# Five heads of one tile's queries moved in among the attention work of three later tiles, with the forget gates cut in two and the gelu issued sooner

## The chip, the core and the metric

The kernel runs on one core of a Trainium2 chip. The core has five engines with a queue of instructions each: TensorE (PE, matrix products into the eight PSUM banks), VectorE (DVE), ScalarE (ACT), GpSimd (POOL, which here issues the gathers) and SyncE (SP, which here issues the loads of weights). Each engine runs its own list in order and stops at a semaphore that isn't there yet. The metric is the device time of one execution in microseconds (us), as a median of several executions.

## The reference

One block of a transformer on 512 tokens of width 1024: two kinds of attention side by side, an output projection, and then, for each token and each of 8 heads, a retrieval of 16 of 16384 single-neuron experts. Cut to what matters:

```python
proj = rmsnorm(x, norm1_g) @ w_in                 # qa, ka, va, forget gates fa, qb, kb, vb
log_f = log_sigmoid(fa + b_f)                     # 8 heads; its running sum biases the logits
out_a = forgetting_attention(qa, ka, va, log_f)   # 8 heads, causal
out_b = differential_attention(qb, kb, vb, lam)   # 4 heads, two maps each, chunk-causal
h = x + concat(out_a, out_b) @ w_out
hn = rmsnorm(h, norm2_g)
q = (hn @ w_q).reshape(tokens, 8, 2, 128)         # per head: two queries of 128
sc = q . sub_keys                                 # 2 x 128 scores; top 16 of each side, then of their 256 sums
eidx, g = 16 experts and their softmax weights    # per token and head
h += sum_k gelu(u[eidx_k] . hn) * g_k * v[eidx_k] # u, v: tables of 16384 rows of 1024
out = rmsnorm(h, final_g)
```

## The kernel before

The 512 tokens are 4 tiles of 128. A head of a tile needs 16 rows of the table u and 16 of v for each token, gathered by POOL: 0.5 MB for each such row of 128 tokens, a "pair" of a u row and a v row being 1 MB. The kernel has three stages.

**Alone.** Tile 0 goes through attention and output projection; then the first three heads (0 to 2) of its queries are made. The list of this stage is BEFORE, which ends with ("keys", 0, 2).

**Hosted.** The retrieval for heads 0 to 6 of tile 0 runs on DVE: for each row a dot product (L1536) and, two groups later, a multiply and add into h (L1572). Woven into it is everything else: the rest of tile 0's queries and the whole attention of tiles 1 to 3 (group 1). A head is 4 groups of 4 rows, and each group has 9 gaps; a place is written here as head.group.gap, so 0.3.3 is gap 3 of group 3 of head 0. In the even gaps 0, 2, 4, 6 DVE does a dot, in the odd ones an add; then every engine does its part of the pieces that the planner has put into that gap. The planner gives each piece a share (share()) and spreads the list `later` over 27 x 9 gaps by the running sum of the shares. In the list of before, heads 3 to 7 of tile 0's queries stand first and the pieces of group 1 behind them.

**Rows.** From head 7 of tile 0 on, u and v come as one 1 MB row each (L710), DVE does the dot alone, ACT makes a diagonal of the weights, and PE adds the rows up (L993). 25 heads of 16 rows go this way.

The pieces that matter here. ("project", 1, s, q): a product with one of the 12 slabs of w_in for tiles 1 to 3; slabs 0 to 3 and 6 to 9 are queries and keys (16 matmuls of 384 columns, L785), 4, 5, 10 and 11 values (a piece for each tile, L777). ("query", 0, c): for an even c a product of h's turned tile with 256 columns of w_q (L777), which ACT copies into `staged`; for an odd c two transposes out of that copy (turn(), L806). ("keys", 0, hd): the scores of head hd (L896). ("forget", 1): PE makes the product with the gates' 8 columns (L836); DVE adds the bias (L1353), takes the magnitude (L1356) and waits for ACT, which does exp and ln, each with a table load of its own (L1164, L1167); then DVE goes on with the decay: subtract, running sum and two copies (L1358 to L1364). ("selq", 1, t) and ("attend", 1, half, step) use that sum: PE makes the scores (L928, L932), DVE adds the mask and finds the maximum (L1440), ACT takes the exponential (L1194), PE turns the map and multiplies it with the values.

ACT's list in the hosted stage has one more thing: the gelu of a group's four dots (L1219), issued in gap 4 of the next group behind the pieces of gaps 0 to 3, and the softmax of the next head's weights (gate_exp, L1211 to L1215) behind group 2. DVE reads the gelu in gap 1 of the group after that (coef, L1562).

Memory that is shared: tile 0's turned h lies in qT, which the projections of group 1 overwrite with their queries, so the queries of tile 0 must come before them. `staged` lies in the right half of mix, which attention writes. The weights come as slabs of 1 MB, in the order of their first use. Slabs 18 to FORE_SLABS go round four places (two of w_ring, two of map_mem), the later ones round the two of w_ring alone; load_slab on SP waits until the slab that was in the place has been used. gfb, the gain of the last norm, is loaded early on SP (L649) and first read behind head 7 of tile 0.

## Time and profile before

| what | before |
|---|---|
| median of 3 executions | 1546.19 us (1545.97 to 1546.67) |
| the profiled execution | 1543.74 us |
| its span, first to last instruction | 1542.0 us |
| mean granted TensorE clock | 0.93 of full |
| busy: PE, DVE, ACT, POOL | 83%, 70%, 30%, 49% of the span |
| moved by the DMA engines | 596.5 MB, mean 387 GB/s |

The span is cut by the stages: tile 0 alone until about 107 us, the hosted stage to about 503 us, the rows behind it. Shares of the whole span are averages over stages with different limits, so the stretches are read one by one: busy time of each engine, and in the last two columns the share of the 16 DMA engines in use and the GB/s. Times within the trace are counted from the first instruction.

### The profile page before, as it was taken

The numbers are of one execution on the slowest core, as the hardware profiler recorded it, in microseconds if no ns is written. First come the engines' busy times: TensorE is split into PE (matmuls) and PEld (weight loads), VectorE is DVE, ScalarE is ACT, GpSimd is POOL, SyncE is SP. The second block draws the span as 40 slices with busy tenths as digits, with TensorE's granted clock in tenths as the row PEclk, the third lists the DMA queues.
The fourth block names the chain that finished last, engine by engine and source line by source line (L and its number), as shares of the span: only waits on it lengthen the run. The fifth ranks groups of instructions, "written<-read, shape, count | busy, mean of one in ns | idle before, by whom it ended". The sixth has DMA issues, their size and how long they took to land.

```text
span 1542.0 us, 13063 instructions
## 1 busy us (share of the span) xinstructions
PE 1278.2 (83%) x3727; PEld 661.2 (43%) x3727; DVE 1078.2 (70%) x2520; ACT 459.6 (30%) x1200; POOL 757.8 (49%) x637
## 2 busy tenths in 40 slices
PE   9999999988888298999776788777787788777777
PEld 8776655665545144444332333332333333333333
DVE  3257699999988776666666676666666776666654
ACT  3432355466233032222222222221222222222212
POOL 0027477775677444454544544444455454444550
PEclk9999999998989599999999998899999999998999
DMA  9669799997999999999999999999999999999995
GB/s 381 260 248 414 277 324 347 374 376 262 350 362 392 400 391 407 423 421 421 422 421 422 421 422 421 421 422 421 421 421 422 422 421 422 422 421 421 421 421 215
DMA packets 99741, 596.50 MB, mean 387 GB/s; under 512 B 11480, under 2 KB 11480, under 8 KB 42328
## 3 DMA queue, kind: packets, MB, share of 16 engines
q0 software_dynamic: 89856, 536.91, 86.1%
q1 hardware_dynamic: 9816, 58.77, 9.5%
q8 instruction: 31, 0.51, 0.1%
q14 instruction: 38, 0.31, 0.1%
...
## 4 chain that ended last, share of the span: by engine, by line
DMA 43%; PE 15%; DVE 6%; POOL 2%; ACT 2%; issue 2%; DVEq 0%; POOLq 0%
PE acc L993 13%; DMA map_mem<-in_peer_uv_dram,eidx 9%; DMA w_ring<-in_peer_uv_dram,eidx 7%; DMA v_all<-in_peer_uv_dram,eidx 7%; DMA act_mem<-in_peer_uv_dram,eidx 6%; DMA mix_mem<-in_peer_uv_dram,eidx 5%; DMA v_ring<-in_peer_uv_dram,eidx 4%; DMA u_ring<-in_peer_uv_dram,eidx 4%; DMA v_ring<-in_peer_v_dram,eidx 2%; PE mm L785 1%; ACT diag L1226 1%; DVE map_mem L1544 1%; DVE w_ring L1544 1%; PE sc L785 1%; POOL v_ring L691 1%
## 5 line engine op out<-in xcount | busy, mean ns | idle before, releaser
L1219 ACT ACTIVATE gel<-hid 128x4 f32<-128x4 f32 x126 | 25.8, 205 | 713.7 <-DVE hid L1544 704.6
L684 POOL DMA_INDIRECT u_ring<-in_peer_u_dram,eidx x112 | 139.7, 1247 | 171.5 <-DVE eidx L1524 98.6
L993 PE MATMUL acc<-v_all,diag 128*128 128x512 f32 x256 | 128.3, 647 | 65.5 <-ACT diag L1226 65.0
L691 POOL DMA_INDIRECT v_ring<-in_peer_v_dram,eidx x112 | 132.3, 1182 | 64.0 <-DVE h L1572 35.4
L1572 DVE SCALAR_TENSOR_TENSOR h<-v_ring,coef,h 128x1024 f32<-128x1024 f32 x112 | 143.9, 1285 | 16.2 <-DMA v_ring<-in_peer_v_dram,eidx 13.0
L1536 DVE CUSTOM_DVE_ANT_0 u_ring<-u_ring,hn 128x1024 f32<-128x1024 f32 x112 | 136.4, 1218 | 14.0 <-DMA u_ring<-in_peer_u_dram,eidx 13.8
L993 PE MATMUL acc<-v_ring,diag 128*128 128x512 f32 x248 | 123.6, 645 | 27.2 <-ACT diag L1226 23.6
L993 PE MATMUL acc<-u_ring,diag 128*128 128x512 f32 x248 | 123.5, 645 | 26.1 <-ACT diag L1226 24.5
L993 PE MATMUL acc<-map_mem,diag 128*128 128x512 f32 x248 | 120.7, 633 | 25.3 <-ACT diag L1226 25.3
L1226 ACT ACTIVATE diag<-ident,coef 128x128 f32<-128x128 f32 x392 | 126.2, 390 | 48.2 <-DVE coef L1562 39.6
L710 POOL DMA_INDIRECT v_all<-in_peer_uv_dram,eidx x64 | 81.0, 1265 | 89.3 <-PE acc L993 81.4
L710 POOL DMA_INDIRECT map_mem<-in_peer_uv_dram,eidx x62 | 74.8, 1207 | 85.2 <-PE acc L993 78.4
L710 POOL DMA_INDIRECT v_ring<-in_peer_uv_dram,eidx x62 | 75.0, 1209 | 79.9 <-PE acc L993 68.2
L993 PEld LDWEIGHTS acc<-v_all,diag 128*128 128x128 f32 x256 | 51.8, 208 | 137.0 <-issue 137.0
L993 PE MATMUL acc<-w_ring,diag 128*128 128x512 f32 x176 | 88.3, 649 | 25.8 <-ACT diag L1226 25.8
L993 PE MATMUL acc<-act_mem,diag 128*128 128x512 f32 x176 | 88.3, 649 | 25.2 <-ACT diag L1226 25.2
L710 POOL DMA_INDIRECT u_ring<-in_peer_uv_dram,eidx x62 | 74.1, 1195 | 69.9 <-PE acc L993 63.4
L1544 DVE CUSTOM_DVE_ANT_0 map_mem<-map_mem,hn 128x1024 f32<-128x1024 f32 x62 | 75.2, 1223 | 46.3 <-DMA map_mem<-in_peer_uv_dram,eidx 46.3
L1544 DVE CUSTOM_DVE_ANT_0 v_all<-v_all,hn 128x1024 f32<-128x1024 f32 x62 | 75.3, 1223 | 45.9 <-DMA v_all<-in_peer_uv_dram,eidx 45.8
L785 PE MATMUL mm<-act_mem,w_ring 128*128 128x384 f32 x304 | 104.1, 498 | 2.9 <-ACT act_mem L1117 2.9
L1544 DVE CUSTOM_DVE_ANT_0 u_ring<-u_ring,hn 128x1024 f32<-128x1024 f32 x60 | 72.8, 1225 | 42.4 <-DMA u_ring<-in_peer_uv_dram,eidx 42.4
L1544 DVE CUSTOM_DVE_ANT_0 v_ring<-v_ring,hn 128x1024 f32<-128x1024 f32 x60 | 72.8, 1224 | 39.8 <-DMA v_ring<-in_peer_uv_dram,eidx 39.8
...
## 6 DMA issues: line engine op xcount, KB each, us to landing
w_ring<-in_slabs_dram SPq DMA_DIRECT2D x29, 1024.0 KB, 8.3
v_ring<-in_slabs_dram SPq DMA_DIRECT2D x6, 1024.0 KB, 11.0
u_ring<-in_slabs_dram SPq DMA_DIRECT2D x6, 1024.0 KB, 11.4
map_mem<-in_slabs_dram SPq DMA_DIRECT2D x6, 1024.0 KB, 8.5
...
```

The lines of the kernel that those rows point to most:

```text
L684: nc.gpsimd.indirect_dma_start(out=u_ring[:, c % U_RING, :], out_offset=None, in_=peer_u[0], in_offset=bass.IndirectOffsetOnAxis(ap=eidx[n ...
L691: nc.gpsimd.indirect_dma_start(out=v_ring[:, c % V_RING, :], out_offset=None, in_=peer_v[0], in_offset=bass.IndirectOffsetOnAxis(ap=eidx[n ...
L710: nc.gpsimd.indirect_dma_start(out=row_mem[place], out_offset=None, in_=peer_uv, in_offset=bass.IndirectOffsetOnAxis(ap=eidx[n % 3][:, c:c ...
L785: last = nc.tensor.matmul(bk[:, 0:n], w[:, c, q * P:(q + 1) * P], actT[:, c, 0:n], start=(c == 0), stop=(c == KC - 1))
L993: last = nc.tensor.matmul(acc[half][:, :], diag[:, c % COLS, :], v_row(n, c)[:, half * BANK:(half + 1) * BANK], start=first, stop=(n % PH ...
L1219: nc.scalar.activation(gel[:, par, g0:g0 + COLS], hid[:, par, g0:g0 + COLS], ACT.Gelu).then_inc(gelu_done, 1)
L1226: nc.scalar.activation(diag[:, c, :], ident[:, :], ACT.Copy, scale=coef[:, par, g0 + c:g0 + c + 1]).then_inc(diag_done, 1)
L1536: nc.vector.tensor_tensor_reduce(out=u_ring[:, c % U_RING, :], in0=u_ring[:, c % U_RING, :], in1=hn[:, :], scale=1.0, scalar=0.0, op0=ALU. ...
L1544: nc.vector.tensor_tensor_reduce(out=u_row(n, c), in0=u_row(n, c), in1=hn[:, :], scale=1.0, scalar=0.0, op0=ALU.mult, op1=ALU.add, accum_o ...
L1572: nc.vector.scalar_tensor_tensor(out=ht, in0=v_ring[:, c % V_RING, :], scalar=coef[:, par, c:c + 1], in1=ht, op0=ALU.mult, op1=ALU.add).th ...
```

## The change

Heads 3 to 7 of tile 0's queries no longer stand ahead of group 1. Each is put among group 1's pieces by itself: head 3 is due at place 0.2, head 4 at 1.2, then 2.2, 3.2 and 4.2, and its two queries and its keys have at least one piece of group 1 between them. For that the turned h of tile 0 gets a home of its own, h0T, laid over gfb, and gfb's load goes to the end of SP's list of slabs, behind a wait for the last of these queries; the copy of a query is written to a new tile own_q instead of `staged`. The slabs of these queries follow in the order of use, so that slabs 20 to 25 are now group 1's first six and the four query slabs of heads 4 to 7 come between group 1's later ones; FORE_SLABS falls from 30 to 26.

"forget" of group 1 is cut into three: ("forget", 1) is PE's product alone and stands ahead of slab 3; ("gate", 1) holds DVE's first two instructions and ACT's exp and ln; ("decay", 1) holds DVE's wait for ACT and the rest. And gelu of the group before is issued in gap 0 instead of gap 4, ahead of the group's pieces.

```diff
-        return {"norm1": 4, "xT": 2, "forget": 6, "mix": 4, ...
+        if kind == "forget":
+            return 6 if p[1] == 0 else 0
+        return {"norm1": 4, "xT": 2, "gate": 6, "decay": 0, "mix": 4, ...
...
-        ps += fox_in[:values_at] + [("forget", g)] + fox_in[values_at:values_at + 1] + [("selq", g, tiles[0])] + fox_in[values_at + 1:]
+        gates = [("forget", g)] if g == 0 else [("gate", g), ("decay", g)]
+        ps += fox_in[:values_at] + gates + fox_in[values_at:values_at + 1] + [("selq", g, tiles[0])] + fox_in[values_at + 1:]
+        if g > 0:
+            ps.insert(ps.index(("project", g, 3, 0)), ("forget", g))
...
-    BEFORE, later = first_pieces[:cut_at], first_pieces[cut_at:] + pieces_of(1)
+    BEFORE, own, later = first_pieces[:cut_at], first_pieces[cut_at:], []
+    total, at = sum(share(p) for p in own + pieces_of(1)), 0.0
+    heads = [[p for p in own if p[0] == "query" and p[2] // 2 == hd] + [("keys", 0, hd)] for hd in range(EARLY_HEADS, PH)]
+    due = [(GRP * (i + 1) - 2) / (SLOTS - 1) for i in range(len(heads))]
+    for p in pieces_of(1):
+        if heads and not heads[0]:
+            heads.pop(0)
+            due.pop(0)
+        if heads and at / total >= due[0]:
+            later.append(heads[0].pop(0))
+            at += share(later[-1])
+        later.append(p)
+        at += share(p)
...
+        h0T = gfb[:, :].rearrange("p (c n) -> p c n", c=KC)
+        own_q = sb("own_q", [P, SLAB])
...
-            sp.dma_start(gfb[:, :], final_g.rearrange("(a n) -> a n", a=1).broadcast_to([P, D])).then_inc(out_done, 16)
             for n in range(N_IN + N_OUT + 2, len(slab_order) - 2):
                 load_slab(n)
+            sp.wait_ge(mm_full, mm_done(("query", 0, 2 * PH - 2)))
+            sp.dma_start(gfb[:, :], final_g.rearrange("(a n) -> a n", a=1).broadcast_to([P, D])).then_inc(out_done, 16)
...
-                        if gap == COLS and (n or grp):
+                        if gap == 0 and (n or grp):
                             gelu(*group_at(GRP * n + grp - 1))
...
-                    from_act(nc.vector.scalar_tensor_tensor(out=e_f[:, 0:n], in0=z_f[:, 0:n], scalar=-1.0, in1=z_f[:, 0:n],
-                                                            op0=ALU.mult, op1=ALU.max), 2)
+                    nc.vector.scalar_tensor_tensor(out=e_f[:, 0:n], in0=z_f[:, 0:n], scalar=-1.0, in1=z_f[:, 0:n],
+                                                   op0=ALU.mult, op1=ALU.max).then_inc(norm_ask, 1)
+                    rooted[0] += 2
+                    if g == 0:
+                        piece("decay", 0)
+                elif kind == "decay":
+                    g, = p
+                    n, t0 = P * len(GROUPS[g]), P * GROUPS[g][0]
+                    dve.wait_ge(act_norm, rooted[0])
```

PE where the hosted stage begins, before: the last of tile 0's queries (the turn out of mix_mem, with keys on either side), the eight products of slabs 0 to 3, the gates' product (with wf), and the values.

```order
L896 MATMUL acc<-subkT,qyT 128x128 x2
L806 MATMUL mm<-ident,mix_mem 128x128 x2
L896 MATMUL mm<-subkT,qyT 128x128 x2
L785 MATMUL acc<-act_mem,map_mem 128x384 x8
L785 MATMUL mm<-act_mem,map_mem 128x384 x16
L785 MATMUL acc<-act_mem,map_mem 128x384 x8
L785 MATMUL mm<-act_mem,w_ring 128x384 x16
L785 MATMUL acc<-act_mem,w_ring 128x384 x8
L785 MATMUL mm<-act_mem,w_ring 128x384 x8
L836 MATMUL mm<-act_mem,wf 8x384 x8
L777 MATMUL acc<-map_mem,act_mem 128x256 x8
```

The same place in the changed kernel, from the last product of BEFORE (w_ring, gfb) on:

```order
L798 MATMUL mm<-w_ring,gfb 128x256 x8
L917 MATMUL acc<-subkT,qyT 128x128 x2
L806 MATMUL mm<-act_mem,map_mem 128x384 x16
L806 MATMUL acc<-act_mem,map_mem 128x384 x8
L806 MATMUL mm<-act_mem,map_mem 128x384 x8
L806 MATMUL mm<-act_mem,w_ring 128x384 x8
L806 MATMUL acc<-act_mem,w_ring 128x384 x8
L827 MATMUL mm<-ident,own_q 128x128 x2
L857 MATMUL mm<-act_mem,wf 8x384 x8
L917 MATMUL acc<-subkT,qyT 128x128 x2
L806 MATMUL mm<-act_mem,w_ring 128x384 x16
L798 MATMUL acc<-map_mem,act_mem 128x256 x8
```

Group 1's first product now follows BEFORE at once; the gates' product stands ahead of slab 3's two products instead of behind them, with the turn and the keys of head 3 around it.

ACT before, from the copy of slab 2's second product on: gate_exp of head 1 (gneg, gexp), two copies, a gelu, a copy, then exp and ln of the gates (e_f), the next gelu, and the first copy of the values.

```order
L1086 ACTIVATE store<-mm 128x384
L1211 ACTIVATE gneg<-top_v 128x1
L1215 ACT_TABLE_LOAD
L1215 ACTIVATE gexp,gsum<-top_v,gneg 128x16
L1086 ACTIVATE store<-mm 128x384
L1086 ACTIVATE store<-acc 128x384
L1219 ACT_TABLE_LOAD
L1219 ACTIVATE gel<-hid 128x4
L1086 ACTIVATE store<-mm 128x384
L1164 ACT_TABLE_LOAD
L1164 ACTIVATE e_f<-e_f 8x384
L1167 ACT_TABLE_LOAD
```

ACT in the changed kernel, from the copies of slab 3 on:

```order
L1107 ACTIVATE store<-mm 128x384 x2
L1232 ACTIVATE gneg<-top_v 128x1
L1236 ACT_TABLE_LOAD
L1236 ACTIVATE gexp,gsum<-top_v,gneg 128x16
L1240 ACT_TABLE_LOAD
L1240 ACTIVATE gel<-hid 128x4
L1185 ACT_TABLE_LOAD
L1185 ACTIVATE e_f<-e_f 8x384
L1188 ACT_TABLE_LOAD
L1188 ACTIVATE e_f<-e_f 8x384
L1102 ACTIVATE v_all<-acc 128x256
```

All copies of slab 3 now stand ahead of gate_exp, gelu and the gates, which follow one another with a table load each.

(A matmul that the order counts once is two records in the trace.)

DVE in the changed kernel from the last dot ahead of the gates on (before, all five instructions of the gates stand in one row behind the add at 1.0.1):

```order
L1564 ISA hid 128x1
L1374 TENSOR_SCALAR z_f<-mm,bf 8x384
L1377 SCALAR_TENSOR_TENSOR e_f<-z_f 8x384
L1590 SCALAR_TENSOR_TENSOR coef<-gel,gate_inv,gexp 128x4
L1600 SCALAR_TENSOR_TENSOR h<-v_ring,coef,h 128x1024
L1564 ISA u_ring,hid<-u_ring,hn 128x1024
L1564 ISA hid 128x1
L1600 SCALAR_TENSOR_TENSOR h<-v_ring,coef,h 128x1024
L1386 SCALAR_TENSOR_TENSOR z_f<-z_f,e_f 8x384
L1389 SCALAR_TENSOR_TENSOR c_all<-ones,c_all,z_f 8x384
```

The gates' first two instructions stand at 0.3.0 and the decay at 0.3.3, with one dot and two adds between them.

Where the later pieces stand: ("attend", 1, 0, 0) was at 1.1.5 and is at 1.0.4; ("attend", 1, 0, 13) was at 2.1.2 and is at 2.0.4; ("attend", 1, 1, 0) was at 3.3.6 and is at 3.3.4; from 4.3.3 on both lists are the same. The products of tile 0's heads 4 to 7 stand at 1.2.3, 2.2.2, 3.2.0 and 4.2.3.

## Rows read from the trace of the kernel before

**Rows 1.** Stretch, us, busy PE PEld DVE ACT POOL (count), clock, DMA share, GB/s.

```profile
107.00:160.00 53.00, 52.16 (x199) 35.56 (x198) 37.58 (x76) 14.05 (x36) 35.08 (x29) 1.00 1.02 407
160.00:180.00 20.00, 20.00 (x74) 12.05 (x73) 6.53 (x11) 9.43 (x17) 2.20 (x4) 1.00 0.65 263
181.00:329.00 148.00, 141.81 (x607) 95.16 (x605) 141.58 (x293) 70.96 (x150) 109.05 (x89) 0.97 0.94 344
...
440.00:460.00 20.00, 16.76 (x44) 9.74 (x45) 14.01 (x21) 9.36 (x23) 12.41 (x12) 0.75 0.90 352
460.00:480.00 20.00, 20.00 (x80) 12.85 (x79) 19.88 (x48) 4.21 (x11) 14.82 (x12) 1.00 1.00 401
...
700.00:800.00 100.00, 83.03 (x195) 36.49 (x194) 66.01 (x157) 24.83 (x69) 51.02 (x45) 0.97 1.01 421
```

**Rows 2.** Timeline of DVE, 0.3.4 to 1.0.4: start, us, instruction [idle before <- releaser].

```profile
150.92 1.21 DVE L1536 CUSTOM_DVE_ANT_0 u_ring<-u_ring,hn 128x1024 f32<-128x1024 f32 x1
...
154.26 1.28 DVE L1572 SCALAR_TENSOR_TENSOR h<-v_ring,coef,h 128x1024 f32<-128x1024 f32 x1 [2.11 <-DMA v_ring<-in_peer_v_dram,eidx]
...
163.94 0.22 DVE L1562 SCALAR_TENSOR_TENSOR coef<-gel,gate_inv,gexp 128x4 f32<-128x4 f32 x1 [4.52 <-ACT gel L1219]
...
172.39 0.60 DVE L1353 TENSOR_SCALAR z_f<-mm,bf 8x384 f32<-8x384 f32 x1 [6.85 <-PE mm L836]
...
175.99 0.55 DVE L1358 SCALAR_TENSOR_TENSOR z_f<-z_f,e_f 8x384 f32<-8x384 f32 x1 [2.42 <-ACT e_f L1167]
...
178.38 1.23 DVE L1536 CUSTOM_DVE_ANT_0 u_ring<-u_ring,hn 128x1024 f32<-128x1024 f32 x1
...
180.73 1.22 DVE L1536 CUSTOM_DVE_ANT_0 u_ring<-u_ring,hn 128x1024 f32<-128x1024 f32 x1
```

**Rows 3.** Timeline of PE around the start of the hosted stage.

```profile
106.53 0.41 PE L806 MATMUL mm<-ident,mix_mem 128*128 128x128 f32 x2
106.78 3.62 PE L777 MATMUL mm<-map_mem,store 128*128 128x256 f32 x16
...
125.57 5.33 PE L785 MATMUL acc<-act_mem,map_mem 128*128 128x384 f32 x16
...
166.95 5.33 PE L836 MATMUL mm<-act_mem,wf 128*8 128x384 f32 x16
```

**Rows 4.** Timeline of ACT: a copy, gate_exp, a gelu and the gates' ln.

```profile
151.57 0.49 ACT L1086 ACTIVATE store<-mm 128x384 f32<-128x384 f32 x1 [4.58 <-PE mm L785]
...
153.68 0.19 ACT L1215 ACTIVATION_READ_ACCUMULATOR gexp<-top_v,gneg 128x1 f32 x1
...
162.40 1.28 ACT L1219 ACT_TABLE_LOAD   x1
163.70 0.20 ACT L1219 ACTIVATE gel<-hid 128x4 f32<-128x4 f32 x1
...
175.44 0.52 ACT L1167 ACTIVATE e_f<-e_f 8x384 f32<-8x384 f32 x1
```

**Rows 5.** Timeline of PE: two of the value products, and the first scores behind them.

```profile
175.76 7.07 PE L777 MATMUL mm<-map_mem,act_mem 128*128 128x256 f32 x32
...
193.67 0.48 PE L928 MATMUL sc<-store 64*128 64x256 f32 x1 [0.47 <-ACT v_all L1081]
```

**Rows 6.** DMA issues from 180 to 330 us: KB each, median us to landing.

```profile
w_ring<-in_slabs_dram SPq DMA_DIRECT2D x6, 1024.0 KB, 8.1
```

**Rows 7.** Timeline of PE: one attention step of the last tile, and the next product.

```profile
290.20 1.12 PE L928 MATMUL sc<-store 64*128 64x512 f32 x2
...
293.45 0.87 PE L777 MATMUL acc<-w_ring,act_mem 128*128 128x256 f32 x3
```

**Rows 8.** Waits of DVE from 449 to 535 us: us in total, times, longest.

```profile
DVE coef L1562 <- ACT gel L1219: 4.7, 1, 4.7
```

**Rows 9.** Chain of work that ended last, 430 to 535 us: start, us, what.

```profile
491.43 10.89 DMA v_ring<-in_peer_v_dram,eidx
```

25 lines of the change are left out of this document (13 added, 12 removed).

## The prediction

> **What bounds the kernel now.** I read the stretches first, for the stage in which the DMA engines are not yet the limit; then the timelines of DVE, PE and ACT where DVE stands still; then the waits and the chain at the stage's end. In the rows stage the DMA share is 1.01 at 421 GB/s [rows 1]: there the time is bytes, and the change moves no byte out of it. In 460 to 480 us, still hosted, it is already 1.00 [rows 1]. So what a change ahead of that is worth is the time by which the gathers reach the same row sooner, less what the DMA engines then still lack.
>
> Ahead of 440 us there are two pictures. From 181 to 329 us three engines are almost full at once: DVE is busy 141.6 of 148.0 us, PE 141.8, and the DMA share is 0.94 [rows 1]. From 160 to 180 us DVE is busy 6.5 of 20 us and the DMA share is 0.65 [rows 1]. The second is a plain loss, and the timeline says whose: DVE waits 4.52 us for a gelu, 6.85 us for the gates' product and 2.42 us for the gates' ln [rows 2], 13.8 us in all. Behind each stands PE. It makes queries of tile 0 from 106.53 to 125.57 us and only then the eight products of slabs 0 to 3 and the gates [rows 3]; ACT's gelu is queued behind the copies of those products. One wait of the same kind comes late: 4.7 us for a gelu [rows 8].
>
> **The front of the hosted stage.** I follow the new order of PE. Tile 0's queries of heads 3 to 7 take 125.57 - 106.53 = 19.04 us [rows 3]. They leave this place, so group 1's first product starts at 106.53. A product of slabs 0 to 3 takes (166.95 - 125.57) / 8 = 5.17 us [rows 3]. Six give 137.55. The 19.04 us hold four products of 3.5 us, the length of one value product [rows 5], and five turns with five keys, so a turn with its keys takes (19.04 - 14.0) / 5 = 1.0 us: 138.55. The gates' product, 5.33 us: 143.9. Two products of slab 3: 154.2.
>
> The gates' first half on DVE stands behind the dot of 0.3.0, two dots and two adds ahead of the dot of 0.3.4 at 150.92 [rows 2], so near 146; the product is ready by then. This wait, 6.85 us, is gone. But ACT's exp and ln stand behind the copies of slab 3, gate_exp and the gelu. From the start of a copy to the end of gate_exp is 153.68 + 0.19 - 151.57 = 2.3 us; a gelu with its table load 1.5 us; exp and ln, each with a load, 2 x 1.8 = 3.6 us [rows 4]. So ln ends at 154.2 + 2.3 + 1.5 + 3.6 = 161.6. DVE is at the decay by about 152: the dot at 150.92 [rows 2] is the next after it, and 1.2 us of the gates now stand ahead. It waits some 9.5 us. **Two of the three waits don't vanish, they are gathered into one.** Queued behind it on DVE are the dots and adds, and POOL's gathers behind these.
>
> The decay takes 178.38 - 175.99 = 2.39 us [rows 2], so DVE is free at 164.0. Before, the work from the dot at 150.92 to the wait for the gates (172.39 - 6.85 = 165.54) less its waits of 2.11 and 4.52 is 8.0 us, and from 178.38 to the end of the dot at 180.73, 3.5 us [rows 2]. That gives 175.5 for the end of the dot at 1.0.4, where before has 181.9. There the first attention step now stands. PE has six value products of 3.5 us first [rows 5], 154.2 + 21.2 = 175.4, then a copy of 0.5 us [rows 4] and two scores of some 0.5 us [rows 5], 1.2 us with the hand-overs, so DVE starts the step at 176.6. **The front gains 181.9 - 176.6 = 5.3 us.** Bounds: 3 us if PE loses a little between its products, 7.5 us if DVE isn't held at 1.0.4.
>
> **The middle.** From here to 329 us both kernels have the same dots and adds, and DVE's work is the same. PE gets three more heads in it (4, 5 and 6), 3 x (3.5 + 1.0) = 13.5 us, but it no longer has the value products that lie behind 181 us before, from 181 to 193.7, 12.7 us [rows 5]. That cancels. DMA does not cancel: with slabs 20 to 25 loaded early for group 1, the four query slabs push group 1's back. By the order of first use and the places, eight slabs are loaded between these two points in the changed kernel (28 to 35 of the list), against five before (32 to 36; the six shown by 330 us [rows 6] less one that starts as the stretch ends), so three more. A slab of 1.05 MB costs 1.05 / (344 / 0.94) = 2.87 us of all 16 engines [rows 1]: 8.6 us. The DMA engines need 0.94 x 148 = 139.1 us before and 147.7 us now. At full share the stretch would stay at 148 us, as long as it is; the share does reach 1.02 over 53 us [rows 1], which would make it 144.8. If instead the idle 8.9 us stay, because they come from the rings of four rows waiting on DVE, it is 156.6. So the middle costs between -3.2 and +8.6 us. I take +2.5: nearer the lower end, since with slabs and gathers together the share stands at 1.00 and 1.02 in two other stretches [rows 1].
>
> In this sum is one new wait of PE. Slab 11 goes into the place of slab 10, and between their products PE has one attention step, 293.45 - 290.20 = 3.25 us [rows 7], and head 6's product, 3.62 us [rows 3]: 6.9 us, where a slab takes 8.1 us to land [rows 6]. That is 1.2 us on PE. Elsewhere two steps, a query's product and its turn and keys lie between, 2 x 3.25 + 3.6 + 1.0 = 11.1 us at the least.
>
> From 329 to 440 us the lists are nearly the same and PE has room (for head 7's two queries): nothing.
>
> **The end of the hosted stage.** The gelu in gap 0 no longer stands behind the first late query, and the wait of 4.7 us [rows 8] goes. What is late next is DMA: the share is 0.90 from 440 to 460 us, which leaves 2.0 us, and 1.00 behind it [rows 1], and the last gathers take 10.89 us to land [rows 9]. So of 4.7 us I count 2.0; bounds 0.5 and 4.7. The gelu ahead of the pieces costs ACT five more table loads in all by the order, 1.28 us each [rows 4]; with ACT busy 71 of 148 us [rows 1] they are hidden, and on a chain of attention steps they would cost 1.28 each. gfb's later load, own_q and h0T move 0.5 MB and no wait: nothing.
>
> **Sum.** -5.3 + 2.5 - 2.0 = -4.8 us. The profiled execution, 1543.74 us (span 1542.0 and 1.7 around it), would be 1538.9; it lies 2.45 us under the median of 1546.19, and the median becomes **1541.4 us**.
>
> **Rivals.** *The middle gives it back.* The three slabs cost their whole 8.6 us, because a share of 0.94 with DVE busy 96% is what such a mixture reaches. For it: all three resources stand at 94 to 96% [rows 1]. Against it: the share of 1.02 with slabs and gathers under way. -5.3 + 8.6 - 2.0 = +1.3: 1547.5, no change to be seen. The Trainium skill, DMA: Bandwidth & Descriptors, "Issuing engines are not separate DMA queues", says that transfers from all queues run on the same 16 engines and interleave, so a slab from SP is paid for by POOL's gathers; that the share passes 1.00 with both under way agrees, and it speaks for this rival.
>
> *The two places of w_ring.* As in the case before, and a slab lands as late as the last gathers do, in 10.89 us [rows 9] instead of 8.1: then PE waits 4.0 us for slab 11 and not 1.2, at a place where PE has no lead over DVE. It decides from a landing of 6.9 us on. +1.3 + 4.0 on top: 1551.5, slower.
>
> *The middle closes up.* Share 1.02, and all of the late gelu counts: -5.3 - 3.2 - 4.7 = -13.2: 1533.0.
>
> *Dearer table switches.* On the new path to the decay ACT changes tables four times in a row (gate_exp, gelu, exp, ln). If a change costs one load more than the rows show, that is 4 x 1.28 = 5.1 us; the front keeps 0.2, and the time is 1546.19 - 0.2 + 2.5 - 2.0 = 1546.5. Against it: the gelu starts 1.30 us after its load does [rows 4]. The Trainium skill, ScalarE: Activation LUTs, "What ACT_TABLE_LOAD costs", puts a drain of about 1.38 us on top of a load of 1.28; as an estimate by that page the path would be 5.5 us longer. The load agrees with the trace, the drain is not in its rows.
>
> **How the numbers follow.** Forecast 0.47, the middle gives it back 0.22, closes up 0.16, w_ring 0.12, dear switches 0.03. A measurement of this kernel can tell about 0.2%, 3.1 us. Faster by more: nine tenths of the forecast and all of closing up, 0.58. Slower by more: w_ring and a little of giving it back, 0.13. Within: 0.29. The range goes from 1534, just above the closed middle, to 1550, short of the w_ring case; that leaves out about half of each, and a little more.
>
> **What would show it.** Right: one wait of DVE of 8 to 13 us for ACT's ln ending near 161.6 us, no wait for the gates' product, the first attention step on DVE near 177 us, the dot of 4.0.0 some 3 us sooner, a DMA share above 0.97 from 177 to 326 us, no wait for a gelu near 450 us. Wrong: PE's six products not closed up from 106.5 us; waits of PE for w_ring by DMA of more than 2 us; a lead at 1.0.4 that is used up by 4.0.0; or a rows stage that doesn't start sooner by the lead.

## The result, and the profile of the changed kernel

The changed kernel is **slower**: 1549.92 us as a median of 20 executions (1545.83 to 1554.22), against 1544.74 us for the kernel before in the same series (1542.56 to 1547.08). The ratio is 1.0035, with a 95% interval of 1.0029 to 1.0042, so 5.4 us. The profiled execution took 1550.56 us with a span of 1548.5 us, 6.5 us over the span before. The forecast was 4.8 us the other way. That the time lies inside the stated range, by 0.1 us, is luck: the range was laid around a median of three executions (1546.19 us) that is 1.5 us above the later one of 20.

Lines of the code stand some 20 to 30 further down than before: the dot is L1564, the add L1600, the attention's maximum L1468, an output product L880.

To see where the time went I took the start of the same dot in both timelines of DVE, place by place. A minus is a lead of the changed kernel. The last row is the seventh dot of the rows stage; the stage's first dot (504.84 us before) is at +5.0.

| place (head.group.gap) | before, us | after against before, us | change since the row above | forecast |
|---|---|---|---|---|
| 1.0.4, the end of the front | 180.73 | -5.2 | -5.2 | -5.3 |
| 3.3.0, the end of the first half's steps | 320.43 | -1.5 | +3.8 | +2.5 |
| 4.2.6 | 378.85 | +2.5 | +4.0 | 0 |
| 5.0.0 | 395.23 | +8.1 | +5.5 | 0 |
| 6.0.0 | 448.74 | +8.3 | +0.2 | 0 |
| the rows stage, seventh dot | 538.36 | +6.6 | -1.6 | -2.0 |

The stretches of the changed kernel, in the order and with the columns of [rows 1]:

```profile
107.00:160.00 53.00, 53.00 (x180) 31.30 (x179) 32.49 (x70) 12.74 (x27) 29.42 (x26) 1.00 0.97 378
160.00:180.00 20.00, 19.53 (x95) 16.63 (x94) 15.32 (x26) 11.11 (x24) 10.52 (x9) 1.00 0.53 182
181.00:329.00 148.00, 140.82 (x599) 94.74 (x597) 137.90 (x289) 74.43 (x158) 107.10 (x88) 0.95 0.96 365
...
440.00:460.00 20.00, 11.30 (x40) 6.75 (x39) 18.43 (x27) 14.26 (x38) 15.73 (x15) 0.74 1.01 401
```

DVE's standstill from 160 to 180 us is gone (15.32 us busy, where [rows 1] has 6.53). But from 181 to 329 us DVE is busy 3.7 us less than before, with the DMA share up from 0.94 to 0.96.

**The front came as forecast.** DVE's timeline, which answers to [rows 2]:

```profile
144.75 0.60 DVE L1374 TENSOR_SCALAR z_f<-mm,bf 8x384 f32<-8x384 f32 x1 [0.56 <-PE mm L857]
...
163.15 0.55 DVE L1386 SCALAR_TENSOR_TENSOR z_f<-z_f,e_f 8x384 f32<-8x384 f32 x1 [12.60 <-ACT e_f L1188]
...
175.49 1.21 DVE L1564 CUSTOM_DVE_ANT_0 u_ring<-u_ring,hn 128x1024 f32<-128x1024 f32 x1
...
177.97 0.42 DVE L1468 CUSTOM_DVE_ANT_0 map_mem<-sc,act_mem 128x256 f32<-128x256 f32 x1 [1.26 <-PE acc L953]
```

One wait for the ln, 12.6 us, has taken the place of three; the dot of 1.0.4 starts at 175.49 instead of 180.73 us; the first attention step stands there and waits for PE.

**The middle is PE's.** Stretches with the columns of [rows 1], from the first product of slab 6 to the end of the last value product; first the changed kernel, then the one before, where PE does the same but for the queries and keys of three heads:

```profile
179.79:324.58 144.79, 139.06 (x587) 93.39 (x585) 135.76 (x282) 72.43 (x154) 105.58 (x87) 0.95 0.96 363
```

```profile
201.18:326.21 125.03, 123.09 (x520) 80.13 (x520) 118.80 (x236) 64.11 (x137) 91.72 (x77) 0.97 0.95 354
```

PE begins 21.4 us sooner and ends 1.6 us sooner. Before, it is busy 123.1 of 125.0 us: it is PE that sets the length here, not one of three. The changed kernel adds 16.0 us of busy time (three heads of some 4.7 us; the other 2 us go with a granted clock of 0.95 against 0.97) and 3.8 us of idle time. What DVE waits for from 177 to 345 us, in the changed kernel (us in total, times, longest):

```profile
DVE u_ring L1564 <- DMA u_ring<-in_peer_u_dram,eidx: 3.9, 3, 2.2
DVE map_mem L1468 <- PE sc L953: 2.6, 2, 2.0
DVE map_mem L1468 <- PE acc L949: 1.8, 1, 1.8
DVE map_mem L1468 <- PE sc L949: 1.4, 1, 1.4
DVE rinv L1476 <- PE o L992: 1.3, 1, 1.3
DVE map_mem L1468 <- PE acc L953: 1.3, 1, 1.3
DVE h L1600 <- DMA v_ring<-in_peer_v_dram,eidx: 0.9, 3, 0.4
```

Together 13.2 us: 8.4 for PE and 4.8 for gathers. The same sum before is 6.2 us: 5.0 for PE and 1.2 for gathers. Three of these waits, `rinv` and the two L949, lie where the second half begins, at 325 to 337 us: the last value product is late and the first steps come behind it.

**Two waits of PE stand in heads 4 and 5.** PE's timeline, and DVE's behind it:

```profile
382.26 0.71 PE L917 MATMUL mm<-subkT,qyT 128*128 128x128 f32 x4 [2.48 <-ACT qyT L1167]
...
397.20 3.56 PE L880 MATMUL acc<-w_ring,store 128*128 128x512 f32 x4 [5.47 <-DMA w_ring<-in_slabs_dram]
```

```profile
387.46 0.69 DVE L1468 CUSTOM_DVE_ANT_0 map_mem<-acc,act_mem 128x512 f32<-128x512 f32 x1 [2.47 <-PE sc L949]
...
402.50 0.69 DVE L1440 TENSOR_TENSOR h<-acc,h 128x512 f32<-128x512 f32 x1 [2.94 <-PE acc L880]
```

The first is head 7's keys: their copy on ACT (`qyT`) stands behind an attention step's exponentials, and the next step's scores stand behind the keys on PE. The second is the output product with slab 13: head 7's query slab sat in its place of w_ring until 4.2.3.

**The end.** The wait of 4.7 us for a gelu [rows 8] is gone (6.0.0 to 6.0.2: +8.3 to +3.5), and the gathers take most of it back (+6.6 at the seventh dot of the rows). DVE's waits from 450 to 550 us:

```profile
DVE h L1600 <- DMA v_ring<-in_peer_v_dram,eidx: 8.6, 5, 4.8
DVE v_all L1572 <- DMA v_all<-in_peer_uv_dram,eidx: 3.1, 2, 1.7
...
DVE coef L1590 <- ACT gel L1240: 2.3, 3, 1.3
```

### The profile page after: what moved, and what is told of

The parts are those of the page before. It is cut to its first block, busy times and chain, and to the rows that moved or that the text cites. A ratio compares the mean times of both kernels' runs of the same rounds, so it can differ in the third digit from the quotient of the medians.

```text
span 1548.5 us, 13067 instructions
## 1 busy us (share of the span) xinstructions
PE 1277.5 (82%) x3727; PEld 662.7 (43%) x3727; DVE 1078.2 (70%) x2520; ACT 466.2 (30%) x1205; POOL 760.2 (49%) x637
## 4 chain that ended last, share of the span: by engine, by line
DMA 42%; PE 17%; DVE 6%; ACT 2%; POOL 2%; issue 1%; DVEq 0%
PE acc L1014 15%; DMA act_mem<-in_peer_uv_dram,eidx 8%; DMA map_mem<-in_peer_uv_dram,eidx 7%; DMA w_ring<-in_peer_uv_dram,eidx 6%; DMA mix_mem<-in_peer_uv_dram,eidx 6%; DMA v_all<-in_peer_uv_dram,eidx 5%; DMA v_ring<-in_peer_uv_dram,eidx 4%; DMA u_ring<-in_peer_uv_dram,eidx 4%; DMA v_ring<-in_peer_v_dram,eidx 3%; PE mm L806 1%; ACT diag L1247 1%; DVE map_mem L1572 1%; PE sc L806 1%; DVE w_ring L1572 1%; DVE h L1600 1%
## 5 line engine op out<-in xcount | busy, mean ns | idle before, releaser
L712 POOL DMA_INDIRECT v_ring<-in_peer_v_dram,eidx x112 | 129.2, 1153 | 63.5 <-DVE h L1600 34.1
L1600 DVE SCALAR_TENSOR_TENSOR h<-v_ring,coef,h 128x1024 f32<-128x1024 f32 x112 | 144.1, 1286 | 16.4 <-DMA v_ring<-in_peer_v_dram,eidx 13.2
L1564 DVE CUSTOM_DVE_ANT_0 u_ring<-u_ring,hn 128x1024 f32<-128x1024 f32 x112 | 136.7, 1220 | 12.1 <-DMA u_ring<-in_peer_u_dram,eidx 11.7
L731 POOL DMA_INDIRECT map_mem<-in_peer_uv_dram,eidx x62 | 78.9, 1272 | 86.9 <-PE acc L1014 77.9
L731 POOL DMA_INDIRECT v_all<-in_peer_uv_dram,eidx x64 | 77.6, 1212 | 86.1 <-PE acc L1014 77.1
L1014 PE MATMUL acc<-act_mem,diag 128*128 128x512 f32 x176 | 85.0, 628 | 24.5 <-ACT diag L1247 24.5
## 6 DMA issues: line engine op xcount, KB each, us to landing
h<-in_x_dram SPq DMA_DIRECT2D x4, 512.0 KB, 12.7
```

Source lines behind the costliest of these rows:

```text
L712: nc.gpsimd.indirect_dma_start(out=v_ring[:, c % V_RING, :], out_offset=None, in_=peer_v[0], in_offset=bass.IndirectOffsetOnAxis(ap=eidx[n ...
L731: nc.gpsimd.indirect_dma_start(out=row_mem[place], out_offset=None, in_=peer_uv, in_offset=bass.IndirectOffsetOnAxis(ap=eidx[n % 3][:, c:c ...
L1014: last = nc.tensor.matmul(acc[half][:, :], diag[:, c % COLS, :], v_row(n, c)[:, half * BANK:(half + 1) * BANK], start=first, stop=(n % PH ...
L1564: nc.vector.tensor_tensor_reduce(out=u_ring[:, c % U_RING, :], in0=u_ring[:, c % U_RING, :], in1=hn[:, :], scale=1.0, scalar=0.0, op0=ALU. ...
L1600: nc.vector.scalar_tensor_tensor(out=ht, in0=v_ring[:, c % V_RING, :], scalar=coef[:, par, c:c + 1], in1=ht, op0=ALU.mult, op1=ALU.add).th ...
```

## The experiments

Each is a change to the kernel before or to the changed one. Times are medians; ratios are to the kernel before, run beside it on the same chip, where it took 1543.6 to 1544.7 us. The table gives for each the start of a dot against before, from the profiled execution; the last place is the seventh dot of the rows stage. One execution is no exact measure: e11 and e15, the same kernel, are up to 4.2 us apart at a place, and e8's profiled execution is 4.6 us under its median.

| run | 1.0.4 | 3.3.0 | 4.2.6 | 5.0.0 | 6.0.0 | rows | median, us | ratio (95%) |
|---|---|---|---|---|---|---|---|---|
| the change | -5.2 | -1.5 | +2.5 | +8.1 | +8.3 | +6.6 | 1549.92 | 1.0035 (1.0029 to 1.0042) |
| e1 gelu alone | +1.1 | -0.8 | +0.3 | +1.8 | +3.7 | +0.5 | 1544.74 | 1.0009 (1.0000 to 1.0017) |
| e2 gates alone | -5.0 | +0.1 | +0.8 | +0.8 | +2.7 | +1.9 | 1543.31 | 0.9994 (0.9985 to 1.0003) |
| e3 queries alone | -7.2 | +4.3 | +9.0 | +15.8 | +16.7 | +15.9 | 1558.04 | 1.0087 (1.0074 to 1.0100) |
| e4 head 7 sooner | -5.0 | -0.3 | +4.6 | +6.2 | +6.6 | +4.1 | 1546.83 | 1.0014 (1.0005 to 1.0023) |
| e5 heads 6, 7 late | -5.6 | -3.3 | -1.2 | +1.7 | +10.3 | +9.4 | 1551.53 | 1.0045 (1.0032 to 1.0058) |
| e6 head 6 later | -4.7 | -2.6 | -0.8 | +4.8 | +5.0 | +3.2 | 1547.97 | 1.0026 (1.0013 to 1.0040) |
| e7 gelu late | -8.1 | +4.5 | +10.0 | +17.0 | +16.9 | +18.3 | 1560.02 | 1.0092 (1.0075 to 1.0110) |
| e8 gates whole | -6.3 | -2.3 | +0.8 | +6.0 | +6.3 | +4.1 | 1551.30 | 1.0046 (1.0033 to 1.0059) |
| e9 thin slabs | -6.3 | -2.0 | +1.5 | +6.8 | +7.0 | +4.9 | 1549.17 | 1.0040 (1.0026 to 1.0054) |
| e10 before, thin slabs | +2.1 | +0.6 | +0.9 | +0.9 | +3.1 | +1.8 | 1545.30 | 1.0002 (0.9993 to 1.0011) |
| e11 head 7 alone | -3.6 | -8.1 | -5.6 | -4.0 | -2.2 | -4.3 | 1541.31 | 0.9989 (0.9975 to 1.0003) |
| e12 heads 6, 7 behind | -2.8 | +1.3 | +3.5 | +6.4 | +9.4 | +6.2 | 1548.15 | 1.0027 (1.0018 to 1.0036) |
| e13 loads spread | -5.6 | -3.1 | +4.9 | +10.6 | +10.8 | +10.2 | 1553.10 | 1.0053 (1.0040 to 1.0066) |
| e14 spread, head 7 sooner | -4.8 | -0.1 | +2.0 | +3.6 | +5.4 | +3.3 | 1546.44 | 1.0018 (1.0009 to 1.0026) |
| e15 as e11 | -3.3 | -4.8 | -3.2 | -1.7 | +0.2 | -0.1 | 1540.90 | 0.9978 (0.9968 to 0.9989) |
| e16 gelu and gates | -13.1 | -0.9 | +0.5 | +2.0 | +3.9 | -0.1 | 1546.62 | 1.0012 (1.0002 to 1.0022) |

(In e2 and e16 the decay stands behind this dot, so their first column says nothing; at 1.0.6 they are at -1.2 and -0.6. Slabs 12 to 15, which the experiments speak of, are the four of the output projection.)

### The three parts apart

**e1.** The kernel before, with

```diff
-                        if gap == COLS and (n or grp):
+                        if gap == 0 and (n or grp):
```

> The kernel before with one part of the change: the gelu issued in gap 0 instead of gap 4. Theory Q (the loss is the work of the moved heads: head 7's query slab holds a place of w_ring that slab 13 of w_in wants, its keys stand right behind the copy they need, and PE has no room for head 6 and 7 in heads 3 and 4): the gelu takes nothing away, its late wait of 4.7 us goes and 2 us of it show at the end, so 1 to 3 us faster than before. Theory G (the early gelu costs: more table loads on ACT, later copies for PE): 2 to 5 us slower than before. Theory D (the middle is full of DMA, and three more slabs pay): no difference, within 2 us.

1.4 us above before by the ratio, the interval from no difference upward. That is within theory D's 2 us; the gain of Q and the 2 to 5 us of G are not found. D's reason, the slabs, is tried in e9. The late wait did go (+3.7 at 6.0.0, -1.1 at 6.0.2), but single microseconds had been lost ahead of it.

**e2.** The kernel before, with the gates' part of the change alone:

```diff
+        gates = [("forget", g)] if g == 0 else [("gate", g), ("decay", g)]
...
+            ps.insert(ps.index(("project", g, 3, 0)), ("forget", g))
```

> The kernel before with one part of the change: the gates' product ahead of slab 3 and the gates cut into three, so that DVE asks ACT two dots earlier. Queries and gelu are as before. All three theories: PE still makes the queries of heads 3 to 7 first, so the product's wait of 6.85 us shrinks while the wait for the gelu and the ln behind it grow; the first attention step still waits for the value products. Between 1 us faster and 2 us slower than before. A gain of more than 3 us would say that the gates alone bring what the front gained.

As expected: 0.9 us under before, and not to be told from none.

**e3.** The changed kernel with gelu and gates as before, so that the queries' move stands alone:

```diff
-                        if gap == 0 and (n or grp):
+                        if gap == COLS and (n or grp):
...
-        gates = [("forget", g)] if g == 0 else [("gate", g), ("decay", g)]
+        ps += fox_in[:values_at] + [("forget", g)] + ...
```

> The changed kernel without the early gelu and without the cut gates: only the queries of heads 3 to 7 moved among group 1's pieces. Theory Q: the costs of the middle and of heads 3 and 4 (together 12 to 13 us in the trace of after from 1.0.4 to 5.0.0) stay, the front gains less than 5 us, and the late gelu waits again: 6 to 12 us slower than before, so slower than the whole change. Theory G: without the early gelu it is at least 2 us faster than the whole change, so 0 to 3 us slower than before. Theory D: as the whole change or up to 3 us slower, 5 to 8 us above before, with the loss in waits for u_ring and v_ring.

13.4 us above before by the ratio, past even theory Q's 6 to 12. The loss is the queries', and the other two parts cure some of it. But the front's lead is 7.2 us here, where Q had less than 5: the cut gates are not what brings it.

**e7 and e8** take one of the two back out of the changed kernel (the first or the second pair of lines of the diff above).

> The changed kernel with the gelu back in gap 4; queries and gates as changed. By the runs of the parts: the gelu alone gave nothing, but the queries alone lost 8 us more than the whole change, with gelus and their table loads behind a query's copy on ACT and ahead of the attention's exponentials. If the early gelu is what cures that, this run is 3 to 8 us slower than the changed kernel. If it is the gates, within 1.5 us of the changed kernel. If the early gelu costs table loads on the path, up to 3 us faster.

> The changed kernel with the gates as before (product behind slab 3, one piece); queries and gelu as changed. In the run with the queries alone the front was 2 us ahead of the changed kernel at 1.0.2 with uncut gates, so the cut gates bring nothing there: expected within 2 us of the changed kernel, either sign. If the cut gates are what makes the difference between queries alone and the whole change, 5 to 8 us slower.

By the ratios the changed kernel is 8.8 us slower still with the late gelu, a little past the 3 to 8 us expected, and 1.7 us slower with whole gates, which can't be told from none. ACT's timeline of e7 shows a place where the gelu matters, and PE's what waits there:

```profile
192.08 1.28 ACT L1240 ACT_TABLE_LOAD   x1
193.38 0.21 ACT L1240 ACTIVATE gel<-hid 128x4 f32<-128x4 f32 x1
193.49 0.37 ACT L1208 ACTIVATE map_mem<-tr 128x256 f32<-128x256 f32 x1
```

```profile
194.00 0.66 PE L970 MATMUL tr<-ident,map_mem 128*128 128x128 f32 x2 [4.15 <-ACT map_mem L1208]
```

The copy of a turned map waits behind the gelu and its table load, and PE behind the copy. In the changed kernel the same gelu runs at 187.26 us, the copy comes right behind its step's exponential at 191.89 us, and PE's pause is shorter:

```profile
192.40 0.66 PE L970 MATMUL tr<-ident,map_mem 128*128 128x128 f32 x2 [2.58 <-ACT map_mem L1208]
```

Behind the pause PE runs at the lower of its two clocks in both kernels (in e7 the granted clock is 1.00 from 188 to 192 us and 0.50, 1.2 GHz, from 196 to 200 us). That is the larger part of the loss: from the dot of 1.0.4 to that of 3.3.0 e7 takes 8.9 us longer than the changed kernel, and PE is busy 5.9 of them with the same products (143.2 us at a mean clock of 0.92, against 137.3 us at 0.95). DVE meets it as scores that come late, with no pause of PE right ahead of them:

```profile
210.91 0.56 DVE L1468 CUSTOM_DVE_ANT_0 map_mem<-sc,act_mem 128x384 f32<-128x384 f32 x1 [4.52 <-PE sc L953]
...
238.22 0.56 DVE L1468 CUSTOM_DVE_ANT_0 map_mem<-acc,act_mem 128x384 f32<-128x384 f32 x1 [4.36 <-PE acc L953]
```

### Where the moved heads stand

**e4, e6 and e5.** The changed kernel with other due places: in e4 head 7 at 4.0.2 to 4.1.0, in e6 head 6 there, in e5 head 6 there and head 7 at 5.2.1 to 5.2.6.

```diff
-    due = [(GRP * (i + 1) - 2) / (SLOTS - 1) for i in range(len(heads))]
+    due = [k / (SLOTS - 1) for k in (2, 6, 10, 14, 16)]      # e4
+    due = [k / (SLOTS - 1) for k in (2, 6, 10, 16, 18)]      # e6
+    due = [k / (SLOTS - 1) for k in (2, 6, 10, 16, 22)]      # e5
```

> The changed kernel with one thing different: head 7's two queries and keys are due so that they come at 4.0.2, 4.0.6 and 4.1.0 instead of 4.2.3, 4.2.x and 4.3.0; their slab is used and released a group sooner, and it stands ahead of slab 12 of w_in in the order of loads. Theory Q: PE's wait of 5.47 us for slab 13 and DVE's 2.94 us behind it go, and the 2.47 us behind the keys too: the dot of 5.0.0 comes 4 to 5 us sooner than in the changed kernel, and the time is 2 to 5 us under it, within 3 us of before. Theories G and D: the same DMA and the same ACT, so within 1.5 us of the changed kernel, 4 to 7 us above before.

From 4.2.6 to 5.0.0 e4 loses 1.6 us instead of 5.5: both waits are gone, and the kernel is 3.2 us faster than the changed one by the ratios, with intervals that don't meet, as theory Q had it. It gives 2.1 us back ahead of that, where this time slab 11 is late on PE:

```profile
310.14 5.41 PE L798 MATMUL mm<-w_ring,act_mem 128*128 128x256 f32 x16 [2.08 <-DMA w_ring<-in_slabs_dram]
```

> The changed kernel with head 6 alone moved, to 4.0.2 to 4.1.0; head 7 stays at 4.2.3 to 4.3.0 with its slab ahead of slab 13. The theory (PE full in 3.x, places of w_ring): no wait of PE for slab 11 and 4.0.4 at 0 to -3 us against before, but the wait of PE for slab 13 of some 5 us stays: the time is 1 to 4 us under the changed kernel. If head 7's slab is the whole cost, it is within 1 us of the changed kernel; if the middle is a matter of DMA, also.

Without head 6's 4.7 us in 3.2, e6 is 3.3 us ahead of the changed kernel at 4.2.6, and PE waits for slab 13 as it does there (5.34 us). The time is 1.4 us under it by the ratios, at the low end of what was expected, but the two intervals overlap.

> The changed kernel with heads 6 and 7 moved to where PE waits for others: head 6's queries and keys to 4.0.2 to 4.1.0 (from 3.2.0), head 7's to 5.2.1 to 5.2.6 (from 4.2.3), among the last output products and norms; their slabs follow in the order of use. What is left of the theory after the first four runs: the changed kernel loses at two kinds of places, where PE is full (heads 2 and 3: each moved head is 4.5 us of PE there, seen as 4.2 us of DVE from 3.3.2 to 4.0.4) and where a query slab keeps a place of w_ring from the next slab (waits of PE of 0.6 to 2.1 us for slab 11 at 3.2 and of 5.5 us for slab 13 at 4.3.7). By it both go here: 4.0.4 starts 1 to 3 us sooner than before instead of 2.7 to 5.4 later, 5.0.0 at least 1 us sooner than before, and the time is 4 to 8 us under the changed kernel, 0 to 4 us under before. Rival M (the middle is at its limit of DMA because three more slabs and the gathers share it): two slabs leave the stretch to 329 us, but the rest stays, so no more than 2 us under the run with head 7 alone moved, 0 to 2 us above before. Rival E (the end takes what the middle gives, since it is bytes there): 5.2.0 is earlier, yet the time is within 1.5 us of before.

This theory fell: 1.5 us above the changed kernel. Up to 5.2.2 the run is ahead of it (+1.4 us against +8.1), though not of before, as expected (5.0.0: +1.7). Then head 7's slab did in another place what it had done to slab 13: it is loaded when slab 14 is done with, at 422 us, and PE stands before it.

```profile
416.78 8.80 PE L880 MATMUL mm<-w_ring,store 128*128 128x512 f32 x16 [3.52 <-DVE h L1440]
430.91 5.22 PE L798 MATMUL acc<-w_ring,gfb 128*128 128x256 f32 x16 [5.33 <-issue]
```

The profile names no releaser ("issue"), but the load issued from 422.2 to 422.5 us with a landing of 8.6 us ends there. DVE's wait behind it:

```profile
DVE h L1440 <- PE mm L880: 8.2, 1, 8.2
```

**e12.** Heads 3 to 5 in front of group 1 as before, head 6 at 4.0.2, head 7 behind the last output product.

```diff
+    later = [p for p in own if of(p) < 6]      # of: the head of a piece
...
+    due = [16 / (SLOTS - 1), 22.6 / (SLOTS - 1)]
```

> Heads 3 to 5 in front as before, head 6 at 4.0.2 to 4.1.0, head 7 at 5.2.6 to 5.3.2, behind the last output product, so that its slab (loaded once slab 14 is done) has 10 us to land; gelu and gates as changed. The front loses 8 us of queries. Theory B: 2.5 MB come later than before, gathers start up to 7 us sooner: between 2 us under and 4 us above before. Rival Q: the middle is free of moved heads up to 4.0, so 5 us or more under before, unless head 7's slab keeps PE as in the run with heads 6 and 7 late (5.3 us idle ahead of its query at 5.2.1, then 8.2 us of DVE): then above before.

4.2 us above before by the ratio, and both expectations had thought its front better: with 8 us of queries less it leads by 2.8 us. DVE waits there 4.1 us for the weights' exponential and 6.9 us for the ln on ACT, and then 4.9 us for one score of PE. PE doesn't wait for head 7's slab, the case in which rival Q had allowed a time above before. From 1.0.4 to 3.3.0, with no moved head ahead of 4.0, the run still loses 4.1 us (columns of [rows 1]):

```profile
177.90:321.75 143.85, 137.22 (x568) 91.40 (x567) 133.31 (x281) 65.67 (x140) 101.31 (x83) 0.93 0.94 349
```

Between the same dots the changed kernel, with three heads more to make, takes 143.5 us with PE busy 137.3 at a clock of 0.95, and the kernel before 139.7 us with 134.3 at 0.96. So PE is busy as long without the three heads as with them, at a lower clock. Why the clock is lower in e12 was not tried further.

### Bytes, or PE's work and the loads' times?

The changed kernel has moved 3.5 MB less by 440 us than before. That suggested that bytes are what counts.

**e9 and e10.** The changed kernel and the one before, with two query slabs cut to a 32nd.

```diff
-                sp.dma_start(slab_mem[place], slabs[sl]).then_inc(slab_in[place], 16)
+                thin = slab_order[n] in ((0, 22), (0, 23))
+                part = KC * SLAB // 32 if thin else KC * SLAB
+                sp.dma_start(slab_mem[place][:, 0:part], slabs[sl][:, 0:part]).then_inc(slab_in[place], 16)
```

> The changed kernel, but of the query slabs of heads 6 and 7 only a 32nd is loaded: the first columns of 1 MB each, so these two heads compute with weights left over from other slabs. All instructions, waits and places stay; 2.0 MB don't move. New theory B (bytes): the traces differ in what the DMA engines have moved by a given time. The changed kernel is 4.4 MB behind before at 180 us, 3.5 MB at 440 and 2.4 MB at 600, which is 5.7 us at 421 GB/s, and that, not DVE's place, decides when the rows stage starts. By it 2.0 MB less give up to 4.8 us: 3 to 5 us under the changed kernel. Rival Q (places of w_ring and PE's room alone): PE's wait for slab 13 stays, since its place still comes free only behind head 7's query, so no more than 1 us under the changed kernel.

> The kernel before with the same two slabs (queries of heads 6 and 7) cut to a 32nd, so these heads compute with left-over weights; nothing else differs. Here the two slabs are loaded in the front, where the DMA engines stand at 0.65 from 160 to 180 us and 0.77 from 180 to 200 us, since DVE holds the gathers up. Theory B: 2.0 MB saved there shorten nothing that ends last: 0 to 2 us under before. If bytes count the same wherever they are saved: 4 to 5 us under before. Rival Q: no difference.

The theory of bytes fell, and the kernel before shows no difference either: 2.0 MB less, both slabs among the loads from 180 to 330 us, bring the changed kernel nothing that can be told (1549.17 against 1549.92 us, 1.0040 against 1.0035; the theory's 3 us would have made it some 1.0016, below e9's interval). From 1.0.4 to 4.2.6 e9 loses 7.8 us, as the changed kernel does, and PE waits for slab 13 all the same:

```profile
395.86 4.50 PE L882 MATMUL acc<-w_ring,store 128*128 128x512 f32 x6 [5.21 <-DMA w_ring<-in_slabs_dram]
```

The Trainium skill, DMA: Bandwidth & Descriptors, "Issuing engines are not separate DMA queues", says that transfers of all queues share the same 16 engines; the longer landings of gathers beside slabs (below) agree. But that a slab therefore costs its time at full rate, as my rival had it, is not what e9 shows.

**e13 and e14.** The changed kernel and e4, with loads of slabs held back so that no two start within 4 us.

```diff
+            LATER_LOADS = {(1, 8): ("project", 1, 7, 0), (1, 10): ("project", 1, 9, 0), (1, 12): ("project", 1, 11, 1)}
...
+                if (g, sl) in LATER_LOADS:
+                    sp.wait_ge(mm_full, mm_done(LATER_LOADS[g, sl]))
```

> The changed kernel, where SP holds three loads of slabs back: slab 8 until the first product of slab 7 is done, slab 10 until the first of slab 9, slab 12 until the second of slab 11. Nothing else differs. In the changed kernel a query's slab is used by one product and gives its place up within 4 us of the slab ahead of it, so two slabs are loaded at once (at 203 and 207 us, at 252 and 256 us), and the gathers of that time land in 9.2 to 9.5 us instead of 6.2 to 6.5; DVE then waits for u_ring and v_ring 4.8 us in all from 210 to 325 us, where before has 1.2. Theory P (pairs of loads): spread out, 2 to 3.6 us of these waits go, 4.0.4 is 2 to 3 us sooner than in the changed kernel, and the time 1.5 to 3.5 us under it. Rival W (PE's work in the middle alone: 3.4 us more of waits for PE): the DMA waits change place but the lead at 4.0.4 is PE's; within 1 us of the changed kernel. Rival L (slabs land too late when held back): a new wait of PE for w_ring, slower.

> The run with head 7 at 4.0.2 to 4.1.0, with loads held back in the same way (slabs 8 and 10 as in the run before this one, and head 7's query slab until the first product of slab 11 is done). Theory P: 1.5 to 3.5 us under the run with head 7 moved alone, so within 1 us of before or up to 2 us under it. Rival W: as that run, 2 us above before.

Neither came out: e13 is 2.8 us above the changed kernel by the ratios, where theory P had a gain and W no difference, and rival L's new wait of PE for a slab is not in the trace. Spreading moves the waits and doesn't remove them. At 2.3.4 e13 is 2.6 us ahead of the changed kernel, as the theory of pairs had it; then the loads that were held back meet the next ones:

```profile
276.80 1.28 DVE L1603 SCALAR_TENSOR_TENSOR h<-v_ring,coef,h 128x1024 f32<-128x1024 f32 x1 [1.70 <-DMA v_ring<-in_peer_v_dram,eidx]
...
288.07 1.23 DVE L1567 CUSTOM_DVE_ANT_0 u_ring<-u_ring,hn 128x1024 f32<-128x1024 f32 x1 [1.18 <-DMA u_ring<-in_peer_u_dram,eidx]
...
325.29 1.28 DVE L1603 SCALAR_TENSOR_TENSOR h<-v_ring,coef,h 128x1024 f32<-128x1024 f32 x1 [4.03 <-DMA v_ring<-in_peer_v_dram,eidx]
...
328.55 1.23 DVE L1567 CUSTOM_DVE_ANT_0 u_ring<-u_ring,hn 128x1024 f32<-128x1024 f32 x1 [1.13 <-DMA u_ring<-in_peer_u_dram,eidx]
```

That is 8.0 us of DVE's waits for gathers, against 4.8 without the holding back. e14 is where e4 is, as rival W had it.

### A version that is faster

**e11, e15 and e16.** The changed kernel with heads 3 to 6 back in front of group 1 and head 7 alone moved, to 4.0.2 to 4.1.0; e15 is the same kernel again. e16 is the kernel before with gelu and gates changed and no query moved.

```diff
+    of = lambda p: p[2] if p[0] == "keys" else p[2] // 2
+    later = [p for p in own if of(p) < 7]
+    at = sum(share(p) for p in later)
...
+    due = [16.2 / (SLOTS - 1)]
```

> The changed kernel with heads 3 to 6 back in front of group 1, as before; head 7 alone is moved, to 4.0.2 to 4.1.0, where the run with head 7 moved there showed no wait of PE for a slab. Gelu and gates as changed. The front is PE's: it gets 4 us of queries less, so the first attention step is 3 to 4 us sooner than before. Theory B: one slab and the last gain (1.5 MB) leave the front and come later, against gathers that start 3 to 4 us sooner: within 1 MB of before at 440 us, and the time 3 us under to 1 us above before, 3 to 8 us under the changed kernel. Rival Q (the middle's PE and places are what costs): no PE work and no slab is added ahead of 4.0, so the lead of 3 to 4 us stays to the end: 3 to 6 us under before.

> The same kernel as in the run with head 7 alone moved (heads 3 to 6 in front, gelu and gates as changed), to narrow its interval. If PE's room in the middle is what the moved heads cost and the front is PE's, it stays 1 to 4 us under before, with the interval below 1.

> The kernel before with the early gelu and the cut gates, no query moved. By the runs of each alone (1 us above and 1 us under before) the sum is none: within 2 us of before. If the run with head 7 alone owes its time to these two and not to the 4 us of PE that head 7 frees in the front, this run is 1 to 4 us under before too.

It is 1.7 us under before in the first series, with an interval that reaches 1.0003, and 3.4 us under in the second, with one that lies below 1. e16 is 1.9 us above before, so the faster kernel owes its time to head 7's move, not to these two. The second series is as expected; the first, short of rival Q's 3 to 6 us, is not clear of no difference. The middle of e11, with the columns of [rows 1] and the same products as in the two stretches above:

```profile
193.29:316.10 122.81, 121.35 (x520) 79.74 (x519) 120.82 (x241) 66.16 (x137) 92.11 (x76) 0.99 0.97 367
```

and what DVE waits for from 177 to 345 us in e11:

```profile
DVE map_mem L1471 <- PE sc L952: 2.1, 1, 2.1
DVE u_ring L1567 <- DMA u_ring<-in_peer_u_dram,eidx: 1.8, 3, 1.4
DVE map_mem L1471 <- PE acc L952: 0.4, 1, 0.4
DVE h L1603 <- DMA v_ring<-in_peer_v_dram,eidx: 0.2, 1, 0.2
```

4.5 us instead of 13.2. With no moved head ahead of 4.0 the front's lead of 3.6 us grows to 8 us at 3.3.0 in e11 (4.8 in e15). From 1.0.4 to 3.3.0 most runs line up by the heads that PE has to make there: with none e11 -4.5, e15 -1.5, e1 -1.8 and e10 -1.6 us; with two (heads 4 and 5) e5 +2.3 and e6 +2.1; with three the changed kernel +3.8, and e4, e8, e9, e13 and e14 between +2.5 and +4.7 (e3 and e7, with the late gelu, +11.4 and +12.7). That would be some 1 to 2 us of DVE's time for each head of 4.7 us of PE.

But a rival goes with it, PE's clock. Over these dots the mean granted clock is 0.99 in e11, 0.98 in e15 and e1, 0.96 before and in e6, 0.95 in the changed kernel, 0.92 in e3 and e7, and 0.93 in e12, which has no such head and yet loses 4.1 us. In the changed kernel the clock falls behind two pauses of PE, 2.58 us at 192 us and 1.94 us at 275 us; before, behind 3.04 us at 199 us and 1.32 us at 238 us. So part of what is put down to the heads, and of what e11 gains, is the clock. e6, at the clock of before, still loses 2.1 us with two heads; beyond that no run parts the two.

## Why the prediction was wrong, step by step

**The front: right.** -5.3 forecast, -5.2 measured; one wait of 9.5 us for the ln forecast, 12.6 found, since DVE came to it 1.5 us sooner and the ln ended at 163.1 and not 161.6 us. Not seen: the cut gates and the early gelu bring none of it. With either taken back the lead is not smaller (e8 -6.3, e7 -8.1; the runs that share the changed kernel's front lie between -4.7 and -6.3), and with both (e3) it is -7.2. What brings it is the queries alone.

**The middle: the step "that cancels" failed.** I set 13.5 us of PE for three heads against 12.7 us of value products that lie behind 181 us before, and called PE's share nil. Both numbers were about right (the three heads took 14.2 us), and PE's start of the middle shows it: 21.4 us sooner at the first product of slab 6. But that head start is used up by the three heads, 2 us at the lower clock and 3.8 us of idle time, and DVE's lead of 5.2 us then has no PE ahead of it to feed it. A busy share of 96% for each of three engines had let me treat them alike; the stretch cut at PE's own products (123.1 of 125.0 us) shows that it is PE that has none to give. The term, up to 329 us, was +2.5 us; measured are +3.8 us to 3.3.0 and +6.7 us to 3.3.6 (328.76 us before). That lies within the bounds I gave (-3.2 to +8.6), near the end that I had not taken, and not for the reason that gave that end: DMA's 8.6 us for three slabs were the upper bound, and with two of the slabs all but taken away (5.7 us at my price) e9 is no faster. For PE's clock I had no term; how much of the 6.7 us is the clock's is open, as said above.

**"From 329 to 440 us nothing": wrong by 6.6 us.** 5.5 of them lie between 4.2.6 and 5.0.0, in the two waits of PE. I had seen that PE has room for head 7 there, and not that a query's slab needs one of two places of w_ring, nor that its keys stand behind a copy on ACT. The rival of w_ring had the mechanism and looked at slab 11 alone: 1.2 us forecast there, 0.6 to 2.1 found in the changed kernel, e3, e4 and e9. The place that decides is slab 13, with 5.5 us on PE and 2.9 us on DVE. I had looked for the shortest stretch of PE's work between a release and a use among the pieces of the middle, and not in the list behind it. e4 takes both waits away and brings 3.2 us.

**The end: right in size.** -2.0 forecast, -1.6 measured from 6.0.0 to the seventh dot of the rows; the gelu's 4.7 us go, and the gathers take 3 us back, at a DMA share of 1.01 from 440 to 460 us.

**The rivals.** The two places of w_ring come nearest in time (1551.5 us) and have half of the mechanism, at slab 13 instead of slab 11; the other half of that sum, the slabs' bytes, is what e9 speaks against, and with it the reason of "The middle gives it back" (1547.5). Dearer table switches are out: see the last section. Of the signs of being wrong two came: a lead used up by 4.0.0 (+4.5 us there), and a wait of PE for w_ring of more than 2 us (5.47).

**What stays open.** Of DVE's 7 us of new waits from 177 to 345 us, 3.4 are for PE and 3.6 for gathers. The runs show that the second part follows neither the bytes of two slabs nor the loads' pairing, since neither cure shortened it as a whole; that it goes with the moved heads is what the order of the runs suggests (with none in the middle 2.0 us in e11, 2.1 in e15 and 1.7 in e12, with two 3.8 in e5 and 4.0 in e6), but no run had the heads' slabs without their products. The heads' own time on PE and the lower clock aren't parted. And why e12's front is poor was only read from its waits.
